# The order of the last attention heads and of the gated delta rule's recurrence in a two-block kernel, on one core of a Trainium2 chip

## What is computed

```python
CHUNK = 64                                   # four chunks of 64 tokens
value = triangular_solve(t_mat, v_beta)
k_cumdecay = triangular_solve(t_mat, k_beta * exp(decay))
def step(S, inp):                            # S: the state, 4 heads x 128 x 128
    qd, kc, val, att, kt, cd = inp
    v_new = val - kc @ S                     # new values
    o = qd @ S + att @ v_new                 # output of the chunk
    S = S * cd + kt.T @ v_new                # new state
    return S, o
...
mixed = concat([rms(o_att) , rms(o_dn) * silu(gate)]) @ w_out
```

## Time and profile before

| what | value |
|---|---|
| median of three executions | 1467.57 us |
| the three executions | 1478.71, 1467.57, 1466.23 us |
| the profiled execution, its own time | 1478.28 us |
| its span, first to last instruction | 1476.5 us |
| mean granted clock of TensorE in it | 0.988 |
| busy: PE, DVE, ACT, GpSimd | 1444.8, 902.0, 722.0, 126.6 us |

### The profile page before, as it was taken

How to read it: one execution, slowest core, us unless ns; L and a number is a source line. 1 busy time by engine, 2 the same in 40 slices (tenths; PEclk the granted TensorE clock), 3 DMA queues, 4 the chain that set the end, 5 groups by cost and what they waited for, 6 DMA issues and landing times.

```text
span 1476.5 us, 21481 instructions
## 1 busy us (share of the span) xinstructions
PE 1444.8 (98%) x7983; PEld 1215.1 (82%) x7983; DVE 902.0 (61%) x1057; ACT 722.0 (49%) x921; POOL 126.6 (9%) x110
## 2 busy tenths in 40 slices
PE   8999999999999999999999999999999899999999
PEld 7888887778888888888888778888888787888887
DVE  6666575757665676666544446656664964476564
ACT  5544455555445454545544434544455752254442
POOL 0000013441000010000000201000001250010000
PEclk9999999999999999999999999999999998799999
DMA  8656655326555655556664345555655411155552
GB/s 260 212 181 191 226 185 172 129 87 200 181 188 185 198 178 192 188 181 202 227 200 171 126 155 174 188 190 182 209 183 178 154 38 61 56 173 200 175 196 86
DMA packets 157771, 253.10 MB, mean 171 GB/s; under 512 B 9824, under 2 KB 101648, under 8 KB 157456
## 3 DMA queue, kind: packets, MB, share of 16 engines
q1 hardware_dynamic: 154736, 247.21, 51.1%
q10 hardware_dynamic: 2976, 5.07, 1.1%
HBM read 251.20 MB, written 1.05 MB: 171 GB/s over the span
## 4 chain that ended last, share of the span: by engine, by line
PE 91%; DVE 4%; ACT 3%; issue 2%; DMA 1%; POOL 0%; SPq 0%; ACTq 0%; DVEq 0%; POOLq 0%
PE bank L1849 14%; PE bank L1851 14%; PE bank L1850 14%; PE bank L1923 13%; PE bank L1920 13%; PE bank L1922 7%; PE bank L1921 7%; ACT w_hi L579 1%; DVE w_lo L1255 1%; PE bank L1861 1%; PE bank L2297 1%; DMA x<-in_x 1%; PE bank L2379 0%; PE bank L2375 0%; PE bank L2359 0%
## 5 line engine op out<-in xcount | busy, mean ns | idle before, releaser
L1255 DVE TENSOR_TENSOR w_lo<-raw,w_hi 128x2048 fp32r<-128x2048 f32 x226 | 517.9, 2293 | 353.1 <-ACT w_hi L579 352.5
L579 ACT ACTIVATE w_hi<-raw 128x2048 fp32r<-128x2048 f32 x229 | 436.9, 1910 | 230.6 <-PE bank L1921 144.5
L1923 PE MATMUL bank<-xT,w_hi 128*128 128x512 f32 x832 | 295.4, 397 | 0.0
L1920 PE MATMUL bank<-xT,w_hi 128*128 128x512 f32 (+1 forms) x848 | 294.4, 393 | 0.0
L1921 PE MATMUL bank<-xT,w_lo 128*128 128x256 f32 (+1 forms) x848 | 234.2, 276 | 0.0
L1922 PE MATMUL bank<-xT,w_lo 128*128 128x256 f32 x832 | 233.7, 281 | 0.0
L1849 PE MATMUL bank<-w_hi,xT 128*128 128x512 f32 x524 | 212.1, 405 | 2.2 <-DVE w_lo L1255 1.7
L1851 PE MATMUL bank<-w_hi,xT 128*128 128x512 f32 x524 | 205.4, 392 | 0.0
L1850 PE MATMUL bank<-w_lo,xT 128*128 128x512 f32 x524 | 204.9, 391 | 0.0
L1851 PE MATMUL bank<-w_hi,hT_lo 128*128 128x512 f32 x484 | 188.7, 390 | 0.0
L1920 PEld LDWEIGHTS bank<-xT,w_hi 128*128 128x128 f32 x848 | 159.3, 188 | 35.5 <-DVE xT L1351 0.3
(11 more groups left out here) (318 smaller groups left out, 1231.0 us busy)
## 6 DMA issues: line engine op xcount, KB each, us to landing
raw<-in_ffn_w_in SPq DMA_DIRECT2D x174, 512.0 KB, 4.7
raw<-in_ffn_w_out SPq DMA_DIRECT2D x88, 512.0 KB, 4.1
raw<-in_w_ff SPq DMA_DIRECT2D x64, 512.0 KB, 4.1
raw<-in_rt_w_in SPq DMA_DIRECT2D x48, 512.0 KB, 4.6
raw<-in_w_in SPq DMA_DIRECT2D x28, 512.0 KB, 4.8
raw<-in_da_w_in SPq DMA_DIRECT2D x24, 512.0 KB, 4.8
raw<-in_rt_w_out SPq DMA_DIRECT2D x16, 512.0 KB, 4.1
raw<-in_da_w_out SPq DMA_DIRECT2D x8, 512.0 KB, 4.0
```

What stands on the lines that cost most here:

```text
L579: act.activation(w_hi[:, n % RING, :], raw[:, n % RING, :], ACT.Copy).then_inc(hi_ready, 1)
L1255: dve.tensor_tensor(w_lo[:, n % RING, :], raw[:, n % RING, :], w_hi[:, n % RING, :].bitcast(F32), ALU.subtract).then_inc(lo_ready, 1)
L1920: pe.matmul(out, hi[:, k, cols], mov, start=first_of, stop=False)
L1923: return pe.matmul(out, hi[:, k, cols], mov, start=False, stop=k == 3)
```

## The change

Four edits, all in `mix()`:

1. TensorE's `recur(n)`: qd @ S goes ahead of the wait for the new values. The wait for ACT's value copies moves from the start of `recur(0)` to its last group; the waits for `k_cumdecay` get a semaphore of their own.
2. DVE's `recur(n)` is taken apart into `new_values(n)` and `new_state(n)` and put in a new order: `new_state(0)`, `att_out(1)`, `new_values(1)`, `new_state(1)`, `new_values(2)`, the attention's norm (line 1801), `new_state(2)`, `new_values(3)`. `new_values(0)` reads bank 4 itself and stands ahead of the `k_cumdecay` copies.
3. The last attention heads: `maxima(6)` and `maxima(7)` go ahead of the last update of the inverse on DVE, `probabilities(7)` ahead of the value copies on ACT; on TensorE `values_2(5)` and `values(6)` go between the values and `k_cumdecay`, `values_2(6)` and `values(7)` ahead of `recur(0)`, `values_2(7)` ahead of `recur(1)`. ACT copies bank 5 first, and bank 4 behind DVE's `new_values(0)`.
4. The first accumulator of the second output block goes ahead of `turn_output(1, ...)`.

```diff
@@ ACT
+                probabilities(7)
                 act.wait_ge(mx_val, 1)
-                for b in range(2):
+                for b in (1, 0):
+                    if b == 0:
+                        act.wait_ge(mx_vnew, 1)
                     act.activation(flat(quarter(dn_val, b)), bank[4 + b][:, :], ACT.Copy).then_inc(mx_valsb, 1)
                 turned_probabilities(6)
-                probabilities(7)
                 turned_probabilities(7)
@@ DVE
-                        dve.wait_ge(mx_valsb, 4)
-                        dve.tensor_copy(dn_vnew[r, :], val).then_inc(mx_vnew, 1)
+                        dve.wait_ge(mx_val, 1)
+                        dve.tensor_copy(dn_vnew[r, :], bank[4][r, :]).then_inc(mx_vnew, 1)
...
-                    maxima(n + 1)
-                maxima(7)
-
-                dve.wait_ge(mx_val, 1)
+                        elif n + 1 == LEVELS:
+                            maxima(6)
+                            maxima(7)
+                    if n + 1 < LEVELS:
+                        maxima(n + 1)
+
+                new_values(0)
+                dve.wait_ge(mx_val, 2)
                 dve.wait_ge(mx_inv, 2 * LEVELS - 3)
-                for b in range(2):
-                    dve.tensor_copy(flat(dn_kcT[b]), bank[6 + b][:, :]).then_inc(mx_valsb, 1)
-                recur(0)
-                recur(1)
+                for b in (1, 0):
+                    dve.tensor_copy(flat(dn_kcT[b]), bank[6 + b][:, :]).then_inc(mx_kc, 1)
+                new_state(0)
                 att_out(1)
-                recur(2)
+                new_values(1)
+                new_state(1)
+                new_values(2)
                 dve.wait_ge(mx_aor, 1)
                 dve.wait_ge(mx_ao, 4)
...
-                recur(3)
+                new_state(2)
+                new_values(3)
@@ TensorE, recur(n)
                         mm.then_inc(mx_KS, 1)
+                        for h in range(4):
+                            at = slice(h * P, h * P + P)
+                            pe.matmul(bank[4 + t][r, at], dn_qhT[:, h, tok], dn_state[(n - 1) % 2][:, at],
+                                      start=h == 0, stop=False)
                     else:
-                        pe.wait_ge(mx_valsb, 4)
-                        pe.wait_ge(mx_qd, 1)
+                        pe.wait_ge(mx_kc, 1)
                     pe.wait_ge(mx_vnew, n + 1)
...
-                    if n:
-                        for h in range(4):
-                            at = slice(h * P, h * P + P)
-                            pe.matmul(bank[4 + t][r, at], dn_qhT[:, h, tok], dn_state[(n - 1) % 2][:, at],
-                                      start=h == 0, stop=False)
+                    if n == 0:
+                        pe.wait_ge(mx_valsb, 2)
@@ TensorE, order
+                mm.then_inc(mx_val, 1)
+                values_2(5)
+                values(6)
                 for u in range(8):
                     for c, r in enumerate(halves):
                         mm = pe.matmul(bank[6 + c][:, u * CHUNK:u * CHUNK + CHUNK], dn_kbe[r, u, :], dn_XT[r, u, :],
                                        start=True, stop=True)
                 mm.then_inc(mx_val, 1)
-                values_2(5)
-                values(6)
-                recur(0)
                 values_2(6)
                 values(7)
+                recur(0)
+                values_2(7)
                 recur(1)
-                values_2(7)
                 recur(2)
-
                 pe.wait_ge(mx_ay, 2)
                 turn_output(0, att_y, 0)
                 recur(3)
                 pe.wait_ge(yT_lo, 8 + 2)
                 out_block(n1, (xT_hi, xT_lo), 0, True, False)
+                out_block(n1 + 1, (xT_hi, xT_lo), 2, False, False, accs=(0,))
                 pe.wait_ge(mx_y, 4)
                 turn_output(1, dn_y, 6)
-                out_block(n1 + 1, (xT_hi, xT_lo), 2, False, False)
+                out_block(n1 + 1, (xT_hi, xT_lo), 2, False, False, accs=(1, 2, 3))
```

More of the change, by code:

```diff
@@ L341, in first_then_second_block @@
         mx_valsb = sem("mx_valsb")
+        mx_kc = sem("mx_kc")
         mx_qd = sem("mx_qd")
@@ L1667, in att_out, with new_values @@
                                           ALU.mult).then_inc(mx_ao, 1)
-                def recur(n):
+                def new_values(n):
                     t, r = n // 2, slice(n % 2 * CHUNK, n % 2 * CHUNK + CHUNK)
-                    val = flat(quarter(dn_val, t))[r, :]
                     if n == 0:
-                        dve.wait_ge(mx_valsb, 4)
-                        dve.tensor_copy(dn_vnew[r, :], val).then_inc(mx_vnew, 1)
-                    else:
+                        dve.wait_ge(mx_val, 1)
+                        dve.tensor_copy(dn_vnew[r, :], bank[4][r, :]).then_inc(mx_vnew, 1)
+                    else:
+                        if n == 1:
+                            dve.wait_ge(mx_valsb, 2)
                         dve.wait_ge(mx_KS, n)
@@ L1678, in recur, with new_state @@
                             dve.wait_ge(mx_O, n - 1)
-                        dve.tensor_tensor(dn_vnew[r, :], val, bank[6][r, :], ALU.subtract).then_inc(mx_vnew, 1)
+                        dve.tensor_tensor(dn_vnew[r, :], flat(quarter(dn_val, t))[r, :], bank[6][r, :], ALU.subtract)\
+                            .then_inc(mx_vnew, 1)
+                def new_state(n):
+                    t, last = n // 2, n % 2 * CHUNK + CHUNK - 1
+                    dve.wait_ge(mx_SU, n + 1)
                     if n == 0:
-                        dve.wait_ge(mx_SU, 1)
                         dve.tensor_copy(dn_state[0], bank[7][:, :]).then_inc(mx_state, 1)
-                    elif n < 3:
-                        dve.wait_ge(mx_SU, n + 1)
+                    else:
                         dve.wait_ge(mx_O, n)
@@ L1688, in recur @@
                             dve.wait_ge(mx_state, 4 * (n - 1) + 1)
-                            decay = dn_exprow[:, 4 * t + h, r.stop - 1:r.stop]
+                            decay = dn_exprow[:, 4 * t + h, last:last + 1]
                             dve.scalar_tensor_tensor(dn_state[n % 2][:, at], dn_state[(n - 1) % 2][:, at], decay, bank[7][:, at],
@@ L2355, in recur @@
                     t, r = n // 2, slice(n % 2 * CHUNK, n % 2 * CHUNK + CHUNK)
+                    tok = slice(t * P + r.start, t * P + r.stop)
                     if n:
+                        if n == 1:
+                            pe.wait_ge(mx_kc, 2)
+                            pe.wait_ge(mx_qd, 1)
                         pe.wait_ge(mx_state, 4 * (n - 1) + 1)
@@ L2370, in recur @@
                         mm.then_inc(mx_SU, 1)
-                    tok = slice(t * P + n % 2 * CHUNK, t * P + n % 2 * CHUNK + CHUNK)
-                    if n:
-                        for h in range(4):
-                            at = slice(h * P, h * P + P)
-                            pe.matmul(bank[4 + t][r, at], dn_qhT[:, h, tok], dn_state[(n - 1) % 2][:, at],
-                                      start=h == 0, stop=False)
+                    if n == 0:
+                        pe.wait_ge(mx_valsb, 2)
                     for h in range(4):
@@ L2487, in mix @@
                     for r in halves:
-                        pe.matmul(bank[4 + u // 4][r, u % 4 * P:u % 4 * P + P], dn_XT[r, u, :], dn_vbeta[r, u, :],
+                        mm = pe.matmul(bank[4 + u // 4][r, u % 4 * P:u % 4 * P + P], dn_XT[r, u, :], dn_vbeta[r, u, :],
                                   start=True, stop=True)
+                mm.then_inc(mx_val, 1)
+                values_2(5)
+                values(6)
                 for u in range(8):
```

## The result

| | before | changed |
|---|---|---|
| median of 15 executions | 1467.67 us | 1460.43 us |
| range of the 15 | 1464.49 to 1478.71 | 1459.85 to 1463.14 |
| the profiled execution | 1478.28 us | 1459.89 us |

The forecast was 1462.5 us; the range held the time, and the gain was undersized: 5.1 us forecast (1467.57 to 1462.5), 7.2 measured. The executions lie in groups. Before: three at 1464.5 to 1464.9, eight at 1466.2 to 1467.9, four at 1475.9 to 1478.7. Changed: eight at 1459.85 to 1460.43, seven at 1461.6 to 1463.1, none higher. A median depends on how many executions fall into each group; by the means (1469.36 and 1461.13) the gain is 8.2 us.

What follows compares the result with a forecast made beforehand. PE, on 91% of the ending chain, was taken as the bound, its low clock costing most. 1478.28 less 12.5 (clock) and 3.9 (order) gives 1461.9, or 1463.0 from 1466.9; 1462.5 us was taken, range 1459.5 to 1469.5.

Steps and rivals of the forecast that it cites:

- The clock: Mixer's recurrence: half clock for 30.60 us from 1241 costs 12.5 us; filling the hole keeps full clock in nearly every execution.
- Rival (a): Around the first state update the clock falls all the same, now in most executions: 1474.5 us, chance 0.12.
- The base: Whole kernel before at full clock: 1465.8 us by the trace, 1466.9 by the mean of the two low executions.
- The order of work: Mixer up to the second output block: at full clock it starts at 1260.1 against 1264.0, 3.9 us less.
- 0.51 for 0.6: Turn of the attention's output: its 0.6 us wait for DVE's norm, at full clock, would be gone.
- 0.54 for 0.7: Second turn, behind the first output block: a 6.2 us chain against 5.45 covered; its 0.7 us wait would be gone.
- Maxima at no cost: DVE ahead of the inverse's last update: moved maxima cost between nothing and 0.2 us; none was taken.
- ACT's new wait at no cost: ACT's bank 4 copy waits some 0.7 us for DVE's; no cost, even if DVE came 1 us late.
- New state as the next to be late: Recurrence: the state takes some 1.3 us with 1.0 of PE's work over it, so 0.3 us comes back, once.
- DVE's norm between new values and state: DVE ahead of new_state(2): the 1.41 us norm fits before the state update ends; if late, up to 1.4 lost.
- (b): Recurrence: the state is the new bound, waits of 0.8 to 1.3 us per step, gain 1.5 to 2: 1465, chance 0.13.
- (c): Behind the mixer: nothing reaches the end, since the weights come no sooner: 1467 us, chance 0.05.

Runs made afterwards that it cites:

- e11: The changed kernel as it is, timed again in the third set: median 1461.97 us (1460.12 to 1463.07), 12 executions.
- e2: Kernel before with two unused full-size matmuls in the 0.79 us wait ahead of the first state update: median 1466.26 us (1464.62 to 1466.92).
- e3: Changed kernel with two extra DVE copies, so TensorE waits 1.10 us ahead of the first state update: median 1465.21 us (1462.93 to 1467.40).
- e9: Changed kernel, retention's wait filled, first edit undone, 1.1 us wait ahead of the first state update put back: median 1477.99 us (1472.65 to 1479.63).
- e5: Changed kernel, retention's wait filled with unused matmuls, first edit undone (qd @ S behind the state update again): median 1462.64 us (1462.35 to 1464.02).
- e8: Kernel before with unused matmuls in both the mixer's 0.79 us wait (two) and the retention's wait (seven): median 1465.06 us (1464.59 to 1466.00).
- e12: Changed kernel with seven unused matmuls in the retention's 2.4 us wait, second timing: median 1460.16 us (1459.90 to 1462.13).
- e1: Kernel before with the first edit alone (qd @ S ahead of the wait for new values): median 1467.74 us (1465.68 to 1470.24), ratio 0.998.
- e6: Changed kernel, retention's wait filled, TensorE's heads back in their old places and att_out(1) behind new_state(1) on DVE: median 1461.23 us (1460.48 to 1462.40).
- e7: Changed kernel, retention's wait filled, fourth edit undone (second output block whole behind the turn): median 1461.16 us (1460.37 to 1461.52).
- e4: Changed kernel with seven unused matmuls in the retention's 2.4 us wait, first timing: median 1460.21 us (1459.93 to 1461.41).

## Why the prediction was right or wrong, point by point

**The clock: right, and the main thing.** "Two of four executions had the low stretch": over the three sets 42 of 101 executions of before lay above 1475. The highest of 27 of the changed kernel (15, and 12 in e11) is 1463.14. e2 shows that filling the hole is enough for that. 12.5 us for the low stretch: the profiled execution, 1478.28, less the 2.15 it had lost earlier, stands at 1476.1 against e2's 1464.63: 11.5 (11.7 at the second output block). The 12.5 was 1 us too large because the layout at full clock was too short: from 1241.45 the prediction has 22.5 us to the second output block, and e2 took 23.40. Rival (a) did not happen. What I hadn't seen is that the change works twice: it takes the hole away, and by taking the waits out of the steps it makes a fall short where one is left (e3 against e9).
On the rules of the Trainium skill that the prediction weighed ("TensorE: Matmul & The Clock Gate"): the one in "A second HAM failure mode: psum-queue depth-cycling", that frequent tiny idles between groups make the clock swing, agrees with e9, where the hole and three waits gave 34.1 us of half clock. With e5 it doesn't agree, where three waits of 0.8 us left the clock up, and in e3 a single wait of 1.10 us was enough for a fall. The price by the section "Terms", 15.3 us, is above the 11.5 measured.

**The base: wrong, and the first failed step.** "At full clock the profiled one would have been 1478.28 - 12.5 = 1465.8, which is ... close to the lowest", and then the mean of the two low executions, 1466.9. I took 1466 to 1468 for the full-clock time. It is 1464.6 (the lowest of before in three sets are 1464.3 to 1464.6, of e2 1464.62, of e8 1464.59). Two terms are missing from the 1465.8: the low stretch in the retention, 3.4 us long and 1.5 us dear in the profiled execution, and the 0.63 at the program's start. The prediction puts both at nothing and gives no reason, although the trace in stretches of 4 us shows the first (the row of 0.73 above); the page's slices of 37 us don't. 1478.28 - 2.15 - 11.5 = 1464.6. Filling the retention's wait takes 1.3 us off the mean (e12 against e11), and e2 against e8 points the same way for the order of before (highest 1466.92 and 1466.00). Of the two low executions, 1466.23 fits one with that stretch; 1467.57 lies above every execution of e2 and probably had a short fall in the mixer as well, which is not shown. My 1462.5 is therefore the time of a changed execution with the retention's stretch (1461.6 to 1463.1), and the median fell into the group without it, by eight executions of 15. In e11 four of twelve were in that group, and the median, 1461.97, was within 0.6 us of the forecast; such a hit would have been luck.

**The least difference that can be told: too coarse.** "About 1%, 14.7 us, is what a measurement can tell from no change." The interval measured is 0.4% wide, and 0.6% is clear of no change.

**The order of work: right in its parts, undersized.** "3.9 us less" measured 4.5 at the second output block (1262.70 in e2; 1259.53 less 1.36 in the changed kernel) and 4.7 at the end (1464.63 less 1459.89), in two profiled executions that begin the mixer at 1230.25 and 1230.26; e8 gives 4.7 to 4.9. The waits were right one by one: 3 x 0.78, 0.51 for 0.6, 0.54 for 0.7, state 0.20 for 0.3, low part 0.22 for 0.15. They sum to 3.79 with `values_2(7)` (0.82), which moved ahead of line 2376 where it covers the hole. The other 0.7 lie in the groups next to a wait: kc @ S to its successor took 0.92 us where matmuls follow, and 1.09 where the wait does (1239.30 to 1241.17 in e2, less 0.78), three times. I had put 1.00 for both. So a wait there costs 0.17 more than its row says; behind att @ v_new it is 0.07 (1242.31 to 1243.60, less 0.20, against 1.02).

**The parts.** Maxima at no cost: right, with 0.47 us to spare. ACT's new wait at no cost: right. New state as the next to be late: right, 0.20. DVE's norm between new values and state: right, and more needed than I wrote: e1 shows that without this order the first edit gives 2.0 us at equal clock and loses 1.6 of them to a fall behind the turn's wait, and e6 that the early heads are what makes the norm's input ready in time (1.0 us). First edit in its place: 2.4 (e5). Fourth edit: 0.4 (e7) for the 0.7 that I had put on the wait before. The chain did not get shorter: from the last att @ v_new to the turn it is 7.28 us in e7 (1251.36 to 1258.64) and 7.29 in e2 (1254.56 to 1261.85). But the first output block starts later behind that group, 1.29 us for 1.02, because of the new wait of 0.22 for the low part, and so covers more of it. Of the signs, one failed: "executions that agree within some 2 us" were 3.3 apart (1459.85 to 1463.14).

**Rivals (b) and (c)** fall: the state's wait is 0.20 us once, and the gain reached the end.

## What to carry to other kernels

When executions of one kernel lie in groups, find the low-clock stretches first, over the whole span and in short pieces, and count every one before a base is taken for the forecast. A short wait can cost many times its length (11.5 us for 0.79 here), and two matmuls whose result nobody uses show that for a few lines of work. Part of a wait that is removed shows up at the next consumer in line unless the other engines' order is changed with it, and a new wait there can bring the clock down and take the gain back (e1).

## What the runs showed of the hardware that I had not expected

- The length of a low-clock stretch depends on what follows the wait it fell behind: behind a wait of 1.10 us it was 3.4 us with a recurrence free of waits (e3) and 34.1 us with three waits of about 0.8 (e9), although PE was counted busy for 31.70 of these. That is one profile of each; the times of all twelve executions of each agree.
- Three waits of about 0.8 us within 12 us leave the clock up (e5), while one hole of 0.79 ahead of the first state update is followed by a fall of some 12 us' cost in 42 of 101 executions of the kernel before. What tells the two places apart was not tried.
- The start of the same program spreads its executions: the same group of four matmuls (line 1949, 1962 in the changed kernel) starts at 22.75 us in e4's trace and at 24.00 in e1's, in part by the first loads and in part by how long the first matmuls ran at half clock (0.63 us for 512 columns up to 16.36 us in e7, 0.40 from 14.63 in e4).
- A group of eight kc @ S matmuls behind which the engine waits takes 0.17 us longer, from its start to the next start less the recorded wait, than the same group with work behind it (1.09 against 0.92); att @ v_new 0.07.
